# A two-layer diffusion trunk on one core: one ordered list of work for all engines, and expert rows in 4 KB halves

## What is computed

```python
def layer(x, cond, lw, rope, ctx_cache):
    sh1, sc1, g1, sh2, sc2, g2 = jnp.split(jax.nn.silu(cond) @ lw['w_mod'] + lw['b_mod'], 6, axis=-1)
    h = rmsnorm(x, lw['g_attn_norm']) * (1 + sc1) + sh1
    mix, new_ctx = branches(h, lw, rope, ctx_cache)
    x = x + g1 * mix
    h = rmsnorm(x, lw['g_ffn_norm']) * (1 + sc2) + sh2
    x = x + g2 * peer(h, lw['w_pq'], lw['peer_keys'], lw['peer_u'], lw['peer_v'])
...
    # peer, for 128 tokens: 8 heads, 2 x 128 keys, 16 of 16384 experts for a head
    sv, si = lax.top_k(sc, P_TOPK)
    cand = sv[:, :, 0, :, None] + sv[:, :, 1, None, :]
    cv, ci = lax.top_k(cand.reshape(t, P_HEADS, 256), P_TOPK)
    gate = jax.nn.softmax(cv, axis=-1)
    act = jax.nn.gelu(jnp.einsum('thkd,td->thk', u_tab[eidx], hb))
    return jnp.einsum('thk,thkd->td', gate * act, v_tab[eidx])
```

## Time and profile before

| | us |
|---|---|
| median of 3 runs (lowest, highest) | 5882.09 (5868.98, 5891.37) |
| profiled execution, span from first to last instruction | 5888.0 |
| PE busy in it | 4851.9 (82%) |
| DVE busy | 3117.5 (53%) |
| ACT busy | 1068.8 (18%) |
| POOL busy | 1547.3 (26%) |
| HBM read | 1503.65 MB, 256 GB/s over the span |

### The profile page before, as it was taken

How to read it: one execution, slowest core, us unless ns; L and a number is a source line. 1 busy time by engine, 2 the same in 40 slices (tenths; PEclk the granted TensorE clock), 3 DMA queues, 4 the chain that set the end, 5 groups by cost and what they waited for, 6 DMA issues and landing times.

```text
span 5888.0 us, 54180 instructions
## 1 busy us (share of the span) xinstructions
PE 4851.9 (82%) x13846; PEld 2304.7 (39%) x13846; DVE 3117.5 (53%) x7277; ACT 1068.8 (18%) x2738; POOL 1547.3 (26%) x1465
## 2 busy tenths in 40 slices
PE   9999999967777777777799999999777777777776
PEld 3578544522222222222235784445222222222222
DVE  2454112176676677676625541122666676676775
ACT  0223100122111211211102220011221121211211
POOL 0200000034334334443302000000333443434443
PEclk9989999999999999999999999999999999999999
DMA  6110111199999999999861002112999999999998
GB/s 260 49 37 1 75 50 72 67 382 372 379 372 368 387 377 386 393 374 381 346 247 57 20 1 75 65 65 100 383 371 388 359 378 379 379 377 387 376 378 338
DMA packets 213890, 1509.10 MB, mean 256 GB/s; under 512 B 24652, under 2 KB 26316, under 8 KB 33996
## 3 DMA queue, kind: packets, MB, share of 16 engines
q0 software_dynamic: 185040, 1344.88, 58.0%
q1 hardware_dynamic: 20880, 141.57, 6.2%
q10 hardware_dynamic: 7800, 20.57, 1.0%
HBM read 1503.65 MB, written 3.28 MB: 256 GB/s over the span
## 4 chain that ended last, share of the span: by engine, by line
PE 44%; DMA 22%; DVE 20%; issue 7%; DVEq 3%; POOL 2%; ACT 1%; ACTq 0%; POOLq 0%
DMA arena<-in_experts,arena 21%; PE ps L473 12%; DVE sq L1299 11%; PE ps L697 7%; PE ps L664 4%; PE ps L645 3%; PE ps L594 3%; PE ps L622 2%; PE ps L656 2%; POOL arena L442 2%; PE ps L493 2%; DVE arena L1202 2%; PE ps L606 2%; DVE arena L1205 1%; DVE arena L1203 1%
## 5 line engine op out<-in xcount | busy, mean ns | idle before, releaser
L697 PE MATMUL ps<-arena 128*128 128x512 f32 x5120 | 2539.0, 645 | 972.0 <-ACT arena L888 934.3
L1299 DVE CUSTOM_DVE_ANT_0 sq<-arena,z 128x1024 f32<-128x1024 f32 x1280 | 1569.8, 1226 | 1024.3 <-DMA arena<-in_experts,arena 957.8
L442 POOL DMA_INDIRECT arena<-in_experts,arena x1280 | 1418.6, 1108 | 2408.2 <-PE ps L697 1980.5
L697 PEld LDWEIGHTS ps<-arena 128*128 128x128 f32 x5120 | 995.3, 203 | 2514.8 <-ACT arena L888 1398.3
L473 PE MATMUL ps<-arena 128*128 128x512 f32 (+3 forms) x1920 | 757.8, 551 | 0.0
L881 ACT ACTIVATE arena<-arena 128x2 f32<-128x2 f32 x640 | 130.1, 204 | 2704.3 <-DVE arena L1299 2704.3
L426 POOL TENSOR_SCALAR ss<-ss 128x1 f32<-128x1 f32 (+3 forms) x86 | 29.7, 345 | 1846.7 <-DVE ss L961 1328.5
L473 PEld LDWEIGHTS ps<-arena 128*128 128x128 f32 x1920 | 364.2, 191 | 370.4 <-issue 336.7
L888 ACT ACTIVATE arena<-ident,arena 128x128 f32<-128x128 f32 x1280 | 439.5, 393 | 128.3 <-DVE arena L1309 127.7
L664 PE MATMUL ps<-arena 128*128 128x128 f32 (+1 forms) x992 | 268.2, 429 | 2.5 <-ACTq L745 2.5
L1119 DVE TENSOR_REDUCE negm<-ps 128x1 f32<-128x768 f32 (+4 forms) x160 | 118.9, 744 | 264.7 <-PE ps L601 164.0
(11 more groups left out here) (166 smaller groups left out, 3447.3 us busy)
## 6 DMA issues: line engine op xcount, KB each, us to landing
arena<-in_weights SPq DMA_DIRECT2D x122, 1024.0 KB, 6.8
arena<-in_experts,arena POOLq DMA_INDIRECT x1280
big<-mod_rows ACTq DMA_DIRECT2D x16, 512.0 KB, 8.6
arena<-in_weights SPq DMA_DIRECT2D x8, 576.0 KB, 4.5
arena<-in_weights SPq DMA_DIRECT2D x4, 768.0 KB, 4.7
arena<-in_weights SPq DMA_DIRECT2D x6, 512.0 KB, 4.2
big<-in_g_norm ACTq DMA_DIRECT2D x4, 512.0 KB, 12.4
x<-in_x_sample POOLq DMA_DIRECT2D x4, 512.0 KB, 5.9
```

The costliest lines, as they stand in the source:

```text
L442: pool.indirect_dma_start(out=ring[s % RING], out_offset=None, in_=ins["experts"], in_offset=bass.IndirectOffsetOnAxis(ap=ihead[:, s:s + 1 ...
L697: last = MM(a[:, c * 512:(c + 1) * 512], diag[s % RING], ring[s % RING][:, D + c * 512:D + (c + 1) * 512], start=False, stop=False)
L1299: last = V.tensor_tensor_reduce(out=sq[:], in0=ring[r][:, 0:D], in1=h2[:, i, :], scale=1.0, scalar=0.0, op0=ALU.mult, op1=ALU.add, accum_o ...
```

## The change

The loops over layers and tiles go. A list `ITEMS` is worked out before the program is written, and each of the five engines walks it from end to end, taking its part of every item. The tiles go through the front in groups: the prompt (0), then all sample tiles for inputs and attention, then tile 1 alone and tiles 2 to 4 together for gates, output and queries. Groups of two expert slots are put between the items of later work, at places that `tensor_cost` spaces out.

```diff
-NU = 5
+NU = 3
+GROUPS = {0: (0,), 1: (1,), 2: (2, 3, 4)}
+def choose(l, t):
+    return [("tk2", l, t, u) for u in range(4)] + [("tkx", l, t), ("tkg", l, t)]
...
+    def group(self):
+        self.items.append(("E", self.dotted))
+        self.dotted += 1
+        if self.dotted - self.weighted > 1:
+            self.weigh()
+        if self.weighted - self.added > 1:
+            self.add()
...
+    def stretch(self, front, groups):
+        total = sum(tensor_cost(i) for i in front)
+        at = put = 0
+        for i in front:
+            while put < groups and at * groups >= (put + 0.5) * total:
+                self.group()
+                put += 1
+            self.items.append(i)
+            at += tensor_cost(i)
...
+def schedule():
+    s = Spread()
+    m = mod_items(0)
+    s.items += [("start",), ("consts", 0)] + m[:8] + prompt_front(0, m[8:]) + [("g2", 0, 0)]
+    s.stretch(sample_first(0), NGRP)
+    s.stretch(merge_and_route(0, 2, GROUPS[2], False) + choose(0, 2), NGRP)
+    s.stretch(choose(0, 3) + choose(0, 4) + [("consts", 1)] + mod_items(1) + prompt_front(1, []), 3 * NGRP)
+    s.flush()
+    s.stretch(sample_first(1), NGRP)
+    s.stretch(merge_and_route(1, 2, GROUPS[2], False) + choose(1, 2), NGRP)
+    s.stretch(choose(1, 3), NGRP)
+    s.stretch(choose(1, 4), NGRP)
+    s.stretch([], NGRP)
+    s.flush()
+    return s.items
```

```diff
-RING = 8
+LEAD = 2
+            table = ins["experts"].rearrange("e (h n) -> (e h) n", h=2)
+            def gather_u(n):
+                l, t = ETILES[n // SLOTS]
+                if n % SLOTS % 32 == 0:
+                    pool.wait_ge(*ready("tk2", l, t, n % SLOTS // 32))
+                if SAME_U[n] is not None:
+                    pool.wait_ge(dot_done, SAME_U[n] + 1)
...
+                gather(n, index_u, UBUF[n])
+            def gather_v(n):
+                if SAME_V[n] is not None:
+                    pool.wait_ge(slot_used, SAME_V[n] + 1)
...
+                gather(n, index_v, VBUF[n])
...
+                gather_u(n)
+                while v <= n - LEAD:
+                    gather_v(v)
+                    v += 1
```

The reciprocal root goes from GpSimd to VectorE, inside each norm:

```diff
-                    nc.gpsimd.tensor_tensor(rstd[:, at:at + cols], ss[:, at:at + cols],
-                                            mhalf[:].to_broadcast([P, cols]), ALU.pow).then_inc(rstd_ready.sem, 1)
+            def root(n, width):
+                a, y, t = ss[:, 0:n], rs[:, 0:n], rt[:, 0:n]
+                TS(a, a, 1.0 / width, EPS, ALU.mult, ALU.add)
+                dve.drain()
+                TS(t.bitcast(U32), a.bitcast(U32), 1, None, ALU.logical_shift_right)
+                dve.drain()
+                TS(y.bitcast(U32), t.bitcast(U32), -1.0, 1597463007.0, ALU.mult, ALU.add)
+                dve.drain()
+                for _ in range(3):
+                    if n == 1:
+                        STT(t, y, rs[:, 0:1], a, ALU.mult, ALU.mult)
...
+                    TS(t, t, -0.5, 1.5, ALU.mult, ALU.add)
...
+                    TT(y, y, t, ALU.mult)
```

The two gelu of a group become a square, a scaled copy and two tanh on ScalarE, the sigmoid of the gates a tanh; the gelu of the gated MLP stays:

```diff
-                                A(gel[:, g * GRP:(g + 1) * GRP], dots[:, g * GRP:(g + 1) * GRP], ACT.Gelu_apprx_tanh).then_inc(gel_ready.sem, 1)
+                    A(dsq[:, c:c + GRP], dots[:, c:c + GRP], ACT.Square, scale=(GELU_A * GELU_B) ** 0.5)
+                    A(dlin[:, c:c + GRP], dots[:, c:c + GRP], ACT.Copy, scale=GELU_A)
+                    act.drain()
+                    for s in range(c, c + GRP):
+                        last = A(dth[:, s:s + 1], dsq[:, s:s + 1], ACT.Tanh, scale=dots[:, s:s + 1], bias=dlin[:, s:s + 1])
```

More of the change, by code:

```diff
@@ L94, in tensor_steps, with attention @@
+def attention(l, tiles):
+    units = [(t, m, h) for t in tiles for m in range(2) for h in range(H)]
+    n = len(units)
+    s = [("qT", l, tiles[0], 0)]
     for u in range(n + 2):
         if u < n:
[L96 removed]
+            s += [("s", l) + units[u]]
         if 1 <= u <= n:
[L98 to L100 removed]
+            s += [("PT", l) + units[u - 1]]
+        if u % H == 4 and u + 4 < n:
+            s += [("qT", l) + units[u + 4][:2]]
@@ L150 @@
[L150 to L183 removed]
+            t, m, h = units[u - 2]
@@ new lines @@
+LOADS = []
+LOAD_NO = {}
+FINAL_ITEM = {}
+for _it in ITEMS:
+    for _b in blocks_of(_it):
+        if _b not in LOAD_NO:
+            LOAD_NO[_b] = len(LOADS)
+            LOADS.append(_b)
+        FINAL_ITEM[_b] = _it
+NEXT_LOADS, SPACE, TURN = {}, [], []
+_lying = [None] * NU
+_turns = [0] * NU
+for _n, _b in enumerate(LOADS):
+    _r = min(range(NU), key=lambda r: -1 if _lying[r] is None else PLACE[FINAL_ITEM[_lying[r]]])
+    if _lying[_r] is not None:
+        NEXT_LOADS.setdefault(FINAL_ITEM[_lying[_r]], []).append(_n)
+    _lying[_r] = _b
+    _turns[_r] += 1
+    SPACE.append(_r)
+    TURN.append(_turns[_r])
@@ L186, in build, with final_slot @@
+LEAD = 2
+def final_slot(bufs, b, l):
+    return max(n for n in range(NSLOT) if bufs[n] == b and ETILES[n // SLOTS][0] == l)
 def build(nc, ins, outs):
@@ new lines, in build @@
+        front = sb("front", [P, FRONT])
+        expert = sb("expert", [P, EXPERT])
+        fr = lambda a, n: front[:, a:a + n]
+        kv_at = lambda a, n: fr(KV0 + a, n)
+        sc_at = lambda a, n: fr(SC0 + a, n)
+        wring = [fr(r * UNIT, UNIT) for r in range(NU)]
+        zt = lambda t: fr(Z0 + 1792 * slot(t), 1792)
+        hT_slot = lambda t: 1 if t == 0 else t - 1
+        hT = lambda t: sc_at(D * hT_slot(t), D).rearrange("p (k n) -> p k n", k=DK)
+        hT_of = lambda ts: sc_at(D * hT_slot(ts[0]), D * len(ts)).rearrange("p (t k n) -> p t k n", t=len(ts), k=DK)
@@ new lines, in build, with take @@
+        qTb = lambda t, m: sc_at(2048 + D * m, D) if t == 0 else sc_at(3088 + D * m, D)
+        otok = lambda t: sc_at(4912, D) if t == 0 else sc_at(5136, D)
+        _e = [0]
+        def take(n):
+            _e[0] += n
+            return expert[:, _e[0] - n:_e[0]]
+        ring = [take(D) for _ in range(7)] + [sc_at(0, D), kv_at(0, D)]
+        diag = [take(P) for _ in range(4)]
+        index_u = [take(SLOTS).bitcast(U32) for _ in range(NT)]
+        index_v = [take(SLOTS).bitcast(U32) for _ in range(NT)]
@@ new lines, in build @@
+        gate = [take(SLOTS) for _ in range(NT)]
+        cand = take(512)
+        tmpk = [take(256) for _ in range(2)]
+        i16f = take(64)
+        cv = take(32)
+        ci = take(32).bitcast(U32)
+        cab = take(64).bitcast(U32)
+        cabf = take(64)
+        sel = take(64)
+        esum = take(16)
+        iota = take(16)
+        dots, dsq, dlin, dth, dgate, wts = (take(8) for _ in range(6))
+        h2_prompt = take(D)
+        g2 = take(D)
+        h2 = lambda t: h2_prompt if t == 0 else zt(t)[:, 0:D]
@@ new lines, in _, with weight, project @@
+            landed = set()
+            def weight(b):
+                if b not in landed:
+                    landed.add(b)
+                    n = LOAD_NO[b]
+                    pe.wait_ge(w_land[SPACE[n]], 16 * TURN[n])
+                return block_in(b)
+            def project(dst, lhs, blocks, cols):
+                for k in range(DK):
+                    w = weight(blocks[k // 4]).rearrange("p (k n) -> p k n", k=4)
+                    last = MM(dst[:, 0:cols], lhs[:, k, :], w[:, k % 4, :], start=k == 0, stop=k == DK - 1)
+                return last
```

2041 lines of the change are left out of this document (1012 added, 1029 removed).

## The result

The changed kernel takes **6247.93 us** (median of 4 runs, 6231.31 to 6256.71) against 5884.93 before in the same session: ratio 1.0615, 95% interval 1.0587 to 1.0644. It is slower by 363 us; the forecast was 6091 and the range 5640 to 6580. The profiled execution's span is 6254.8 us.

The account below looks back on a forecast made before the run. TensorE bounds the fronts and DMA the expert stretches, with no overlap between them. Start, two layers' sample stretches, layer edge and tail sum as 450 + 2 x (951 + 635) + 1340 + 1129 = 6091 us; range 5640 to 6580.

Parts of the forecast that it names:

- A: In each layer, sample inputs to tile 1's choice, with 64 groups of expert slots beside: 951 us, TensorE alone 782.
- B: In each layer, tiles 2 to 4 through gates and queries, with 64 groups of expert slots: 635 us.
- P: Everything before the first expert slot, including the first front: about 450 us, between 400 and 560.
- the inputs: Sample tiles' input part within A: VectorE's 318 us and some latency, 325 us.
- the attention: Sample tiles' attention within A: 370 us, including 19 for the missing pair bank and 14 for the ScalarE copy.
- T: Last three tiles' experts alone, 384 slots at GpSimd's 2.85 us, plus 20 for choice pieces, 15 at the end: 1129 us.
- C: Layer's edge (choice of tiles 3 and 4, conditioning, layer 1's prompt) under 192 groups: DMA's 1258 us plus hops, 1340 us.
- Rival 2: GpSimd becomes the bound, its gathers delayed by dots, 3.15 to 3.6 us a slot: 6390 us; chance 0.12.
- Rival 3: 4 KB rows run at 21.3 GB/s an engine, rows in C and T taking 16% more: 6370 us; chance 0.09.
- Rival 1: Queues absorb the waits; A and B follow TensorE, C and T follow DMA: 5630 us, faster; chance 0.29.
- rival 4: No overlap: dots waiting for rows hold all queues, a slot costing 2.77 us also in A and B: 6610; chance 0.07.
- The estimate from a page: Skill's transfer-time fit: two halves 6.4 us against 4.4 for one block, T 1.45 times as long, near 6600 in all.

Follow-up runs that it names:

- experiment 4: Kernel after without its 2560 gathers, slots working on seven constant buffers; 5465.05 us.
- experiment 5: Kernel after with only the first 12 us piece of each tile's choice left in place, the other three moved between later work; 6251.3 us.
- experiment 8: Kernel of experiment 5 with each piece of the choice cut into four items of about 3 us, slot groups between them; 6058.79 us.
- experiment 2: Kernel before with each slot's row fetched in two gathers of 4 KB halves, same eight buffers; 6241.14 us.
- experiment 12: Kernel before with two gathers a slot as in experiment 2, the second moving only 512 bytes of each row; 6262.19 us, ratio 1.0643.
- experiments 1, 3 and 8: On the kernel after: 1 drops the root's three refinement steps, 6094.55 us; 3 cuts repeated weight loads to 128 columns, 6116.45 us; experiment 8 has its own line.
- experiment 9: Kernel after with spread choice in quarter pieces, full 8 KB rows in the last three tiles and two root refinement steps; 5918.58 us, ratio 1.0053.
- experiment 11: Kernel of experiment 9 with a shorter reciprocal root and each choice piece in seven parts of 0.9 to 2.1 us; 5850.99 us, ratio 0.9949.

## Why the prediction was right, and where it was not

- **The sign and the mechanism** hold: DMA-bound tiles did go under TensorE-bound work (experiment 4: 31 us of waits for rows in A and none in B, where the kernel before paid 2.77 us a slot), and it was given back at the pitch of the gathers, in VectorE's inputs and in the choice.
- **P, A and B** came to 3623 us for 3622; that it agrees to 1 us is luck, as the five differ by up to 13 us and some of their terms by more. Inside A two terms were off and cancelled: the inputs, 342 and 341 us from the first dot to the first maximum of scores for 325, where the root's pitch was as I had taken it, but 7 us of latency were too few; and the attention, 351 and 348 for 370, so that the missing bank and the copy on ScalarE, which no run takes apart, cost some 13 us together by what is left of the sum, not 33.
- **T, +69.** The slot was right in size: "2 x 1.41 = 2.82, and I take 2.85", and the last tile shows 370/128 = 2.89. Some of that is luck: GpSimd's own time is 2.67 there, as its mean issue is 1.05 us and not 1.11, and waits for used slots make up the rest. GpSimd as the bound is shown in the kernel before with two gathers, and in T it isn't parted from the DMA engines at 97%. The step that failed is "plus 20 for pieces of 12 us of choice in front of the dots": the two tiles with pieces take 44 and 29 us more than the last, 73 in all. That is 9 us for each of the eight pieces, where the 20 is 2.5 and has no working. A piece in one stretch stops the dots, and behind them the slots, the release of buffers and the gathers: one moved into T by experiment 5 costs 14 us, and quarters (experiment 8 against 5) give 70 us back in T.
- **C, +93.** The step that failed is "DMA sets it: 403 + 75 MB at 380 GB/s". After the choice DMA runs at 357 GB/s, which over 1150 us is 70 us. The pitch of 2.82 us, which I had used in T, I had left out here, where DMA's 95% looked like the bound. Quarter pieces give back 21 us, thin weights 62, no gathers 273. GpSimd is at 701 + 645 x 0.30 = 895 of those 1150 us, so it isn't the bound alone; how C's remaining loss divides between issues, bytes and the order of the list stays open.
- **The rivals.** Rival 2's mechanism is what acts in the kernel before with two gathers, at a smaller size: its 3.15 to 3.6 us a slot needed every other gather of a first half to be hit, and the mean issue is 1.05 us in T's last tile, 1.10 in experiment 2. Rival 3's rate of 21.3 GB/s an engine isn't met: it is 23.0 in experiment 2 and 361/(16 x 0.97) = 23.3 in T's last tile, against 24.65 for 8 KB rows, and experiment 12 shows that the bytes don't set the slot in the kernel before. Rival 1 asked for hops under 258 us; experiments 1, 3 and 8 alone give back 153, 131 and 189. Experiment 4 excludes rival 4.
- **The estimate from a page.** The fit 2.0 us + bytes/436e3 stands in the Trainium skill (DMA: Bandwidth & Descriptors) in the section "Anatomy of one DMA — SWDGE (gpsimd) path", and not in "Bandwidth"; the estimate of 1.45 for two halves isn't met, as a slot went from 2.77 to 3.03 us in experiment 2.
- **The signs that I named.** The first dot (437) and A (955) came as written. VectorE was 72% busy in the input part (247.55 of 342 us) and not over 85%; DMA stood at 70% until 2213 us and only then at 94%; a slot of T took 1183/384 = 3.08 us over all, and 2.89 only in the last tile; and in T the DMA engines were the fuller, at 92% against GpSimd's 87% with its gaps. The dots in T waited 482 us for rows, with GpSimd mostly busy and not idle.
- **Function tables.** I had counted nothing for them, "if tanh and exponential need no switch". They need none: the loads fall from 99 to 9, which frees 116 us of ScalarE; no run shows what this is worth in the whole.
- **Where the gain went.** The two gathers cost 339 us in the kernel before, the refinement steps 153, the repeated weights 131, the whole pieces 189. Together they are more than the 363 us of the loss. Within the kernel after the parts nearly add up: experiment 9 gives back 329, where its parts sum to 189 + 95 (full rows in T) + a third of 153 = 335. The 339 is another kernel's, in which all 1280 slots lie bare, and may not be added to them. So that the overlap by itself is worth several hundred us is my reading, and no run has it with whole rows everywhere. What is shown is that smaller pieces of the choice, whole rows in T and a shorter root take the kernel after from 6248 to 5851 us, 0.5% under the kernel before.

## What to carry to other kernels

Halving what one gather brings doubles the issues, and where the issuing engine takes 1.1 + 0.3 us for one, twice that, 2.80 us here, is a floor of the slot beside that of the bytes, even where the queues' busy share is 94%; so halve rows only where the stretch has other work above that floor. Where work is spread by one ordered list, keep each item shorter than the slack of the thing beside it: the same VectorE operations cost 193 us less in quarters (experiment 8 against 5). And a chain of tiny dependent operations is priced by its pitch, not by its length.

## What the runs showed of the hardware that I had not expected

- A DMA share of 94% with 346 GB/s was no proof of a DMA bound. With 192 GB/s and 64% in its place the slot took 3.07 us for 3.03.
- With eight buffers of 8 KB rows and one gather a slot, the DMA engines reach 397 GB/s at 99% in the last tile (experiment 11). The kernel before had 379 at 96% with buffers of the same size and number; why it stays below isn't shown.
- Tanh and exponential follow each other on ScalarE without a load of a function table, while gelu and exponential each bring one, 1.28 us. In the kernel before 48 loads stand at the experts' gelu and 40 at the choice's exponential. In the kernel after these are the only loads but one:

```profile
L1002 ACT ACT_TABLE_LOAD x4 | 5.1, 1283 | 0.1
L1030 ACT ACT_TABLE_LOAD x4 | 5.1, 1283 | 0.1
```

- Idle time of TensorE costs again behind it. The 8 records at 2053.27 us, after 5.24 us of idle time, take 6.68 us, or 0.84 each, where one took 0.44 in a full front; the granted clock between 2053 and 2060 us is 0.55, so nearly all of it at 1.2 GHz.
